# First three attentions: V as 64-column weights, the two heads of a pair on the two column halves, gates projected by channels, outputs left as operand

## The chip, the core and the metric

One core of a Trainium2 chip runs the whole program. TensorE (PE) multiplies: one operand is loaded into the array as weights, the other streams past it column by column. VectorE (DVE), ScalarE (ACT) and GpSimd (POOL) do the elementwise work, SyncE (SP) issues the loads. Each engine works through its own list in order; semaphores tie the lists together. The metric is the device time of one execution in microseconds, the median of several.

## The reference

Two blocks follow each other on 512 tokens of width 1024. The first has a context of 256 more tokens. Its layers, cut to what matters here:

```
# layer 1 (ab): h = adaln(x), hc = adaln(ctx); pp = h @ w_in, split into cq, ckv, kr, gq, gk, gv, gate
# "mla": 8 heads, 96 dims for q and k, 64 for v        "gqa": 8 heads of 64, 2 kv heads
oa = joint_dense_attention(qa, ka, va, kac, vac)        # keys: 256 context + 512 tokens
ob = joint_dense_attention(qb, kb, vb, kbc, vbc)
mix = concat([oa, ob]) * silu(g)                        # 1024 channels, context rows too
x = x + gate * (mix @ w_out)
# layer 2 (cd): "win": 8 heads of 64, 2 kv heads, a window of 3 blocks of 128 beside the context, a sink
oc = joint_window_attention(q, k, v, kc, vc, sink)      # 512 channels
od = gb * short_conv(gcv * gh, conv_w)                  # 512 channels
x = x + gate * (concat([oc, od]) * silu(g) @ w_out)

def block(qi):                                          # one attention, one block of 128 queries
    p = softmax(einsum('bqkgd,bnkd->bkgqn', qi, kk) * d ** -0.5)
    return einsum('bkgqn,bnkd->bqkgd', p, vv)
```

The second block (two more layers with the attentions "diff", "fox" and "odd", and embeddings) isn't touched.

## The kernel before

Tokens stand in tiles of 128: tiles 0 to 3 are the sequence (XT), 4 and 5 the context (CT). The program is a row of stages: in1 and up (projections), the attentions gqa and mla, out1, in2, the attention win, out2, in3, and on to the end. The modulation of later layers (modb, 32 small products of 32-row results) runs between the units of gqa and mla.

A projection is a list of chunks of up to 512 columns. A chunk's weights come in units of two slabs of 128 rows; ACT rounds a unit to a high part (L1341), POOL makes the low part (L2197), and `tile_product` (L966 to 985) does three matmuls for each slab and tile: high by high, high by low, low by high (L982 to L984). In the row form tokens are weights and the columns of w stream; in the col form columns of w are weights and 512 tokens stream, so that the result has channels on its partitions. Before, only col_b, col_c, col_h and col_z of in2 are in the col form. `turn_group` (L942) turns rows into operand columns by transposes (L949), ACT writes their high part (L1406), DVE the low one (L1813).

An attention (`attention` on each engine: L1149, L1466, L1948) is a loop over units, one head and one tile of queries. gqa and mla have 48: in each head the tiles 0, 4, 1, 5, 2, 3. A unit of tiles 0 to 3 has 768 keys (six blocks, here a large unit), one of tiles 4 and 5 has 256 (two blocks, a small unit). win has 32 units of 512 or 640 keys. Step j of the loop:

- PE: scores of unit j (L1190 and L1191, in mla L1193 to L1195) into banks 0 and 1 or 2 and 3; transposes for the operands of the next heads (L1145); transposes of the probabilities of unit j-1 (L1218), the first half of the blocks to bank 4, the rest to bank 5; the product with V of unit j-2 (L1230); then a step of modb if one is due (L1080, L1089). The weights of L1230 are the turned probabilities, 128 columns; what streams is a block of V, 64 columns, in fp32.
- DVE: the minimum of the scores (L1966, in win L1969), the low parts of operands (L1888), the copy of bank 4 (L1980), 1/sum (L1986), and result times 1/sum times gate into rows of rz (L1992).
- ACT: the exponential with its sum (L1491), and the copy of bank 5 (L1502).

Banks 4 and 5 have one buffer each: the transposes of a unit wait for the copies of the unit before it. After mla the rows in rz are turned by 48 transposes of 128 by 128 for out1 (m1), after win by 16 for out2 (m2). Two tiles of the next stage (`lead_tile`) stand among the last units to fill the array's time.

The order is written out by hand in the loops and in tables by step number.

## Time and profile before

| what | us |
| --- | --- |
| median of 3 runs | 1586.86 (1584.73 to 1588.18) |
| the profiled execution, its own time | 1588.51 |
| its span, first to last instruction | 1586.6 |
| TensorE busy in it | 1522.5 (96%) |

The profile lists each engine's busy time, the chain of work that ended last, and the instructions in order of time with what they waited for. A matmul's row runs from its start to the modelled end of its result; the next one on the array starts sooner, so what a group of matmuls occupies is read from its start to the start of the next row. An fp32 matmul stands as two records; a transpose and an fp32r matmul as one.

### The profile page before, as it was taken

Reading aid. Unit: us, or ns where it says so; the run is one execution under the profiler, and the core shown is the slowest. Engines: PE = TensorE matmul, PEld = TensorE weight load, DVE = VectorE, ACT = ScalarE, POOL = GpSimd, SP = SyncE. Lnnn points to the kernel's source line nnn. Section 1 sums busy time; section 2 is a strip of 40 time slices with the busy share of each in tenths; the row PEclk is TensorE's granted clock in tenths of the full one; section 3 lists DMA queues with packets and bytes.
Section 4 is the critical chain, followed back from the end, with each engine's and each line's share of the span. In section 5 each row is a group of like instructions: output and inputs, shape, how many; then the busy total and the mean of one; then the engine's idle time right before and its main releaser. Section 6 shows DMA issues by size and latency. Waiting matters only on the chain.

```text
span 1586.6 us, 24812 instructions
## 1 busy us (share of the span) xinstructions
PE 1522.5 (96%) x9192; PEld 1299.9 (82%) x9192; DVE 895.5 (56%) x2041; ACT 663.4 (42%) x1351; POOL 571.8 (36%) x333
## 2 busy tenths in 40 slices
PE   5999999999999999999999999987999999999998
PEld 3788978998998878888888889965788788877887
DVE  4575787666665265943752798046321599717312
ACT  3322354445554353335643424457423433336332
POOL 1232235900001553446705444421344444430244
PEclk9999999999999999999999999999999999999999
DMA  9421213331013242331003323300123233310322
GB/s 327 118 66 55 74 55 94 95 94 41 28 41 120 90 123 80 93 97 49 28 15 95 87 90 91 94 27 28 50 84 103 80 97 102 93 54 1 98 89 93
DMA packets 102630, 128.60 MB, mean 81 GB/s; under 512 B 10544, under 2 KB 60656, under 8 KB 102512
## 3 DMA queue, kind: packets, MB, share of 16 engines
q1 hardware_dynamic: 102512, 127.01, 26.4%
q8 instruction: 76, 1.25, 0.3%
q14 instruction: 42, 0.34, 0.1%
HBM read 124.90 MB, written 2.10 MB: 80 GB/s over the span
## 4 chain that ended last, share of the span: by engine, by line
PE 87%; DVE 6%; issue 3%; ACT 2%; DMA 1%; POOL 1%; SPq 1%; DVEq 0%; ACTq 0%; POOLq 0%
PE psum L982 20%; PE psum L984 20%; PE psum L983 20%; PE psum L1230 8%; PE psum L1218 4%; PE psum L949 3%; PE psum L1145 2%; PE psum L1190 1%; PE psum L1080 1%; PE psum L1197 1%; PE psum L1193 1%; PE psum L1191 1%; PE psum L1195 1%; PE psum L1194 1%; DVE psum L1910 1%
## 5 line engine op out<-in xcount | busy, mean ns | idle before, releaser
L2197 POOL TENSOR_TENSOR wlo<-wraw,whi 128x1024 fp32r<-128x1024 f32 (+4 forms) x177 | 411.6, 2326 | 906.2 <-ACT whi L1341 906.2
L1341 ACT ACTIVATE whi<-wraw 128x1024 fp32r<-128x1024 f32 (+4 forms) x177 | 180.5, 1020 | 459.3 <-PE psum L984 453.1
L982 PE MATMUL psum<-whi,h2h 128*128 128x512 f32 (+2 forms) x800 | 309.5, 387 | 2.5 <-DVE h2l L1813 1.5
L984 PE MATMUL psum<-whi,h2l 128*128 128x512 f32 (+2 forms) x800 | 305.2, 381 | 0.0
L983 PE MATMUL psum<-wlo,h2h 128*128 128x512 f32 (+2 forms) x800 | 304.6, 381 | 0.0
L982 PE MATMUL psum<-whi,hTh 128*128 128x512 f32 (+2 forms) x500 | 192.2, 384 | 3.5 <-DVE hTl L1813 2.4
L984 PE MATMUL psum<-whi,hTl 128*128 128x512 f32 (+2 forms) x500 | 186.9, 374 | 0.0
L983 PE MATMUL psum<-wlo,hTh 128*128 128x512 f32 (+2 forms) x500 | 186.6, 373 | 0.0
L982 PEld LDWEIGHTS psum<-whi,h2h 128*128 128x128 f32 x800 | 150.3, 188 | 28.4 <-issue 2.7
L984 PEld LDWEIGHTS psum<-whi,h2l 128*128 128x128 f32 x800 | 150.2, 188 | 27.1
L983 PEld LDWEIGHTS psum<-wlo,h2h 128*128 128x128 f32 x800 | 150.4, 188 | 24.7
L1491 ACT ACTIVATE pr<-psum,nmax 128x256 f32<-128x256 f32 (+6 forms) x160 | 113.3, 708 | 92.2 <-DVE nmax L1966 76.4
L982 PEld LDWEIGHTS psum<-whi,hTh 128*128 128x128 f32 x500 | 95.1, 190 | 19.7 <-issue 3.3
L984 PEld LDWEIGHTS psum<-whi,hTl 128*128 128x128 f32 x500 | 94.9, 190 | 16.6
L1966 DVE TENSOR_REDUCE nmax<-psum 128x1 f32<-128x768 f32 x96 | 74.9, 780 | 57.7 <-PE psum L1195 31.3
L983 PEld LDWEIGHTS psum<-wlo,hTh 128*128 128x128 f32 x500 | 95.3, 191 | 14.5
L1218 PE MATMUL psum<-ident,pr 128*128 128x128 f32 x672 | 102.6, 276 | 3.5 <-ACT pr L1491 3.2
L1230 PE MATMUL psum<-gq,prT 128*128 128x64 f32 x736 | 91.1, 269 | 0.0
L1230 PEld LDWEIGHTS psum<-gq,prT 128*128 128x128 f32 x736 | 88.5, 192 | 0.3 <-issue 0.2
L1218 PEld LDWEIGHTS psum<-ident,pr 128*128 128x128 f32 x672 | 76.0, 141 | 13.6 <-ACT pr L1491 10.1
L1980 DVE COPY prT<-psum 128x256 f32<-128x256 f32 (+2 forms) x160 | 73.1, 457 | 5.3 <-PE psum L1218 4.7
L1992 DVE SCALAR_TENSOR_TENSOR rz<-psum,rinv,rz 128x64 f32<-128x64 f32 (+1 forms) x160 | 47.5, 297 | 40.9 <-PE psum L1230 38.1
(321 smaller groups left out, 2609.9 us busy)
## 6 DMA issues: line engine op xcount, KB each, us to landing
wraw<-mod_w_in SPq DMA_DIRECT2D x32, 512.0 KB, 3.8
wraw<-w_in_odd_in SPq DMA_DIRECT2D x32, 512.0 KB, 3.7
wraw<-cd_w_in_in SPq DMA_DIRECT2D x24, 512.0 KB, 3.7
wraw<-w_in_even_in SPq DMA_DIRECT2D x20, 512.0 KB, 3.8
wraw<-ab_w_in_in SPq DMA_DIRECT2D x16, 512.0 KB, 4.0
wraw<-ab_w_out_in SPq DMA_DIRECT2D x16, 512.0 KB, 3.7
wraw<-w_ple_gate_in SPq DMA_DIRECT2D x16, 512.0 KB, 3.8
mod_w_even<-mod_w_in SPq DMA_DIRECT2D x8, 512.0 KB, 10.4
```

The source lines that it names most:

```text
L949: mm = eng.transpose(psum[:, b, n_ * P:(n_ + 1) * P], turn[name]["rows"](t, k), ident[:, :])
L982: eng.matmul(dst, a[0], ww[0], start=first, stop=False)
L983: eng.matmul(dst, a[0], ww[1], start=False, stop=False)
L984: mm = eng.matmul(dst, a[1], ww[0], start=False, stop=last_)
L1218: mm = eng.transpose(psum[:, bk, (b - b0) * P:(b - b0 + 1) * P], pr[:, i % 2, b * P:(b + 1) * P], ident[:, :])
L1230: mm = eng.matmul(psum[:, 6, 0:dv], prT[:, i % 2, n_ * P:(n_ + 1) * P], v_rows(name, h, b), start=n_ == 0, stop=n_ == len(bl) - 1)
L1341: eng.activation(hi_of(u)[:, :, 0:w], wraw[:, u["id"] % RAW, :, 0:w], ACT.Copy).then_inc(*to("split_hi", u["id"]))
L1491: eng.activation(pr[:, j % 2, 0:w], psum_flat[:, s0 * 512:s0 * 512 + w], ACT.Exp, bias=nmax[:, j % 4:j % 4 + 1], scale=-1.0, accum_out=rsu ...
L1966: eng.tensor_reduce(m, sc, AX.X, ALU.min).then_inc(*note("nmax", (name, j)))
L1980: eng.tensor_copy(prT[:, i % 2, 0:nb * P], psum[:, 4, 0:nb * P]).then_inc(*note("probs_a", (name, i)))
L1992: eng.scalar_tensor_tensor(out=dst, in0=o, scalar=ri, in1=dst, op0=ALU.mult, op1=ALU.mult)\
L2197: eng.tensor_tensor(lo_of(u)[:, :, 0:w], wraw[:, u["id"] % RAW, :, 0:w], f32(hi_of(u)[:, :, 0:w]), ALU.subtract)\
```

## The change

In gqa, mla and win the units are now taken by pairs of heads: head h and head h+1 of the same tile stand side by side in the list. `column_attention` takes the place of `attention` for these three:

- In the product with V, the weights are a block of V (64 columns), and the turned probabilities stream (128 columns). Head h writes partitions 0 to 63 of bank 6, head h+1 partitions 64 to 127, block by block in turn. The result has channels on its partitions. So 1/sum must lie along the columns: two more fp32 matmuls for each pair (L1300, 1/sum repeated over 64 weight columns, the identity streams) write it beside the result.
- DVE then does two multiplications of 128 by 128 per pair (gate times 1/sum, times result) in place of two of 128 by 64, and one reciprocal of two columns.
- PE turns the probabilities two steps after their scores (one before) and does the product with V of a pair at every second step, four steps after the pair's first scores. There are three buffers for probabilities and for turned ones. Bank 4 takes two blocks (three before), bank 5 up to four.
- The queries of two heads are turned by one transpose of 128 columns (two of 64 before), in gqa and win.
- The gates of layer 1 are projected by channels (form "both": 512 sequence tokens, then 256 context tokens stream past weight columns), as three chunks of 384, 384 and 256 columns, and those of win by the col form. The result of the attention is multiplied in place, and is the operand: the transposes of m1 and m2 are gone. ACT copies the high part of a pair's 128 channels (`mix_hi`, 8 of 128 by 768 and 4 of 128 by 512), POOL subtracts for the low part (`mix_lo`).
- out1 and out2 take their slabs in the order 0, 4, 6, 2 in the first chunk. After the last unit of mla nothing is turned.
- Where mla starts, eight operands are prepared ahead (four before).

```diff
         def units_of(name):
-            if name in ("gqa", "mla"):
-                return [(h, t) for h in range(8) for t in (0, 4, 1, 5, 2, 3)]
+            if name in COLUMNS:
+                return [(h, t) for h0 in range(0, 8, 2) for t in ((0, 4, 1, 5, 2, 3) if name != "win" else XT) for h in (h0, h0 + 1)]
...
# TensorE
+            def column_attention(name):
...
+                for j in range(n_units + 3):
...
+                    if (name, j) in LEAD_COLUMNS:
+                        lead_tile(*LEAD_COLUMNS[name, j])
+                    if 2 <= j < n_units + 2:
+                        turn_probs(name, j - 2, probs(name, j - 2))
+                    m, r = divmod(j - 4, 2)
+                    if m >= 0 and r == 0:
+                        h, t = units[2 * m]
+                        for e in range(2):
+                            copies_ready(name, 2 * m + e)
                         bank_free(6)
-                        for n_, b in enumerate(bl):
-                            mm = eng.matmul(psum[:, 6, 0:dv], prT[:, i % 2, n_ * P:(n_ + 1) * P], v_rows(name, h, b),
-                                            start=n_ == 0, stop=n_ == len(bl) - 1)
+                        for n_, b in enumerate(bl):
+                            for e in range(2):
+                                eng.matmul(psum[64 * e:64 * e + 64, 6, 0:P], v_rows(name, h + e, b),
+                                           turned_probs(name, 2 * m + e)[:, n_ * P:(n_ + 1) * P], start=n_ == 0, stop=n_ == len(bl) - 1)
+                        eng.wait_ge(*at("vector", ("inverse", name, m)))
+                        for e in range(2):
+                            col = rinv[:, 2 * (m % 4) + e:2 * (m % 4) + e + 1].broadcast_to([P, 64])
+                            mm = eng.matmul(psum[64 * e:64 * e + 64, 6, P:2 * P], col, ident[:, :], start=True, stop=True)
...
# VectorE
+            def column_attention(name, beside=lambda j: None):
...
+                for j in range(len(units) + 4):
+                    if j < len(units):
+                        maximum(name, j)
+                    m, r = divmod(j - 5, 2)
+                    if m >= 0 and r == 0:
+                        z = gate_columns(name, m)
+                        eng.wait_ge(*at("product_v", (name, m)))
+                        eng.tensor_tensor(z, psum[:, 6, P:2 * P], z, ALU.mult).then_inc(*small())
+                        after_last()
+                        eng.tensor_tensor(z, psum[:, 6, 0:P], z, ALU.mult).then_inc(*note("mixed", (name, m)))
+                    m, r = divmod(j - 3, 2)
+                    if m >= 0 and r == 0 and m < len(units) // 2:
...
+                        eng.reciprocal(rinv[:, r_:r_ + 2], rsum[:, c_:c_ + 2]).then_inc(*note("vector", ("inverse", name, m)))
+                    if 2 <= j < len(units) + 2:
+                        copy_probs(name, j - 2, turned_probs(name, j - 2), (name, (j - 5) // 2) if j >= 5 else None)
...
# ScalarE
+            def column_attention(name):
...
+                        exponentials(name, j, probs(name, j))
+                    if 2 <= j < len(units) + 2:
+                        copy_probs(name, j - 2, turned_probs(name, j - 2), (name, (j - 5) // 2) if j >= 5 else None)
...
+                    if (name, j) in MIX_HI:
+                        mix_hi(*MIX_HI[name, j])
```

On TensorE, in gqa, a small unit's step before: scores of unit j, transposes of the large unit j-1, the product with V of the small unit j-2 (L1230), modulation (L1089). kTs and qTs are the keys and queries of gqa, pr and prT the probabilities and the turned ones:

```order
L1190 MATMUL psum<-kTs,qTs 128x256 [waits exps]
L1191 MATMUL psum<-kTs,qTs 128x256
L1218 MATMUL psum<-ident,pr 128x128 [waits probs_a,exps]
L1218 MATMUL psum<-ident,pr 128x128 x2
L1218 MATMUL psum<-ident,pr 128x128 [waits probs_b]
L1218 MATMUL psum<-ident,pr 128x128 x2
L1230 MATMUL psum<-gq,prT 128x64 [waits mixed,probs_a]
L1230 MATMUL psum<-gq,prT 128x64
L1089 MATMUL psum<-sel,mod_row 128x2 [waits mod_rows]
```

And an even step of the changed kernel: scores of a small unit j, transposes of the large unit j-2 (L1238), the product with V of the small pair j-4, j-3 (L1295), its 1/sum (L1300), modulation (L1152); rx is a third buffer of turned probabilities:

```order
L1271 MATMUL psum<-kTs,qTs 128x256 [waits exps]
L1272 MATMUL psum<-kTs,qTs 128x256
L1238 MATMUL psum<-ident,pr 128x128 [waits probs_a,exps]
L1238 MATMUL psum<-ident,pr 128x128
L1238 MATMUL psum<-ident,pr 128x128 [waits probs_b]
L1238 MATMUL psum<-ident,pr 128x128 x3
L1295 MATMUL psum<-rx,gq 64x128 [waits mixed,probs_a]
L1295 MATMUL psum<-prT,gq 64x128
L1295 MATMUL psum<-rx,gq 64x128
L1295 MATMUL psum<-prT,gq 64x128
L1300 MATMUL psum<-ident,rinv 64x128 [waits vector]
L1152 MATMUL psum<-wraw,silu_pad 32x128 [waits evac_dve,load_w1]
```

The product with V is now in every second step only, and the transposes of unit j-2 still wait (probs_a) for DVE's copy of unit j-3.

On VectorE, in gqa, two steps before:

```order
L1966 TENSOR_REDUCE nmax<-psum 128x1 [waits evac_dve,scores]
L1980 COPY prT<-psum 128x256 [waits product_v,probs_turned]
L1986 RECIPROCAL rinv<-rsum 128x1 [waits exps]
L1992 SCALAR_TENSOR_TENSOR rz<-psum,rinv,rz 128x64 [waits product_v,vector]
L1966 TENSOR_REDUCE nmax<-psum 128x1 [waits mixed,scores]
L1980 COPY prT<-psum 128x384 [waits product_v,probs_turned]
```

and two steps of the changed kernel, even and odd:

```order
L2104 TENSOR_REDUCE nmax<-psum 128x1 [waits evac_dve,scores]
L2115 COPY rx<-psum 128x256 [waits product_v,probs_turned]
L2104 TENSOR_REDUCE nmax<-psum 128x1 [waits probs_a,scores]
L2128 TENSOR_TENSOR rz<-psum,rz 128x128 [waits product_v]
L2130 TENSOR_TENSOR rz<-psum,rz 128x128 [waits vector]
L2135 RECIPROCAL rinv<-rsum 128x2 [waits exps]
L2115 COPY prT<-psum 128x256 [waits product_v,probs_turned]
```

In an odd step two multiplications and the reciprocal now stand between the minimum and the copy; before, the copy came right behind the minimum.

## Rows read from the trace of the kernel before

**Rows 1.** Stretches: us, busy (instructions) of PE, PEld, DVE, ACT, POOL, clock, DMA, GB/s.

```profile
225.40:363.40 138.00, 134.41 (x1325) 120.55 (x1323) 96.56 (x253) 67.80 (x174) 67.67 (x77) 1.00 0.32 93
363.40:505.90 142.50, 140.45 (x1196) 131.76 (x1196) 92.73 (x232) 73.62 (x174) 4.76 (x2) 1.00 0.19 60
736.00:821.50 85.50, 80.75 (x676) 76.49 (x674) 60.89 (x174) 54.10 (x148) 45.57 (x32) 1.00 0.04 14
509.40:514.70 5.30, 5.30 (x15) 4.17 (x14) 0.69 (x1) 0.60 (x1) 0.00 (x0) 0.51 0.00 0
1040.00:1072.00 32.00, 25.44 (x146) 17.40 (x144) 19.92 (x70) 19.59 (x58) 5.59 (x5) 1.00 0.00 1
```

**Rows 2.** In order of time, TensorE in gqa: start, us, what, xrecords.

```profile
300.50 0.38 PE L1218 MATMUL psum<-ident,pr 128*128 128x128 f32 x2
300.72 1.45 PE L1230 MATMUL psum<-gq,prT 128*128 128x64 f32 x12
302.10 0.65 PE L1080 MATMUL psum<-wraw,silu_pad 128*32 128x128 f32 x16
302.68 0.38 PE L1190 MATMUL psum<-kTg,qTs 128*128 128x256 f32 x1
...
303.01 0.81 PE L1218 MATMUL psum<-ident,pr 128*128 128x128 f32 x6
303.67 0.56 PE L1230 MATMUL psum<-gq,prT 128*128 128x64 f32 x4
304.06 0.34 PE L1089 MATMUL psum<-sel,mod_row 128*128 128x2 f32 x2
304.26 0.48 PE L1190 MATMUL psum<-kTg,qTs 128*128 128x512 f32 x1
...
305.04 0.38 PE L1218 MATMUL psum<-ident,pr 128*128 128x128 f32 x2
```

**Rows 3.** The same, in mla.

```profile
412.01 1.45 PE L1230 MATMUL psum<-cq,prT 128*128 128x64 f32 x12
413.26 0.48 PE L1193 MATMUL psum<-kTh,qTh 96*128 96x512 f32 x1
...
414.41 0.82 PE L1218 MATMUL psum<-ident,pr 128*128 128x128 f32 x6
```

**Rows 4.** The same, VectorE in gqa, beside Rows 2.

```profile
300.70 0.96 DVE L1966 TENSOR_REDUCE nmax<-psum 128x1 f32<-128x768 f32 x1 [0.56 <-PE psum L1191]
301.58 0.41 DVE L1980 COPY prT<-psum 128x256 f32<-128x256 f32 x1
301.91 0.15 DVE L1986 RECIPROCAL rinv<-rsum 128x1 f32<-128x1 f32 x1
...
303.21 0.42 DVE L1966 TENSOR_REDUCE nmax<-psum 128x1 f32<-128x256 f32 x1 [0.65 <-PE psum L1191]
```

**Rows 5.** Two lines of code on VectorE: ns min/median/max, first and last start, forms.

```profile
L1992 DVE SCALAR_TENSOR_TENSOR rz<-psum,rinv,rz x160: 282/284/352, 233.8 to 1478.0; 128x64 f32<-128x64 f32 x128, 128x128 f32<-128x128 f32 x32
L1888 DVE TENSOR_TENSOR kTl<-psum,kTh x16: 411/554/689, 359.6 to 471.8; 96x512 fp32r<-96x512 f32 x8, 96x256 fp32r<-96x256 f32 x8
```

**Rows 6.** In order of time: TensorE waits for VectorE, start of gqa.

```profile
227.37 0.68 DVE L1888 TENSOR_TENSOR qTs<-psum,qTs 64x512 fp32r<-64x512 f32 x1
...
228.20 0.65 PE L1080 MATMUL psum<-wraw,silu_pad 128*32 128x128 f32 x16 [1.49 <-DVE qTs L1888]
```

**Rows 7.** In order of time, TensorE in win, a unit of five blocks.

```profile
748.36 0.36 PE L1190 MATMUL psum<-kTs,qTs 128*128 128x256 f32 x1
...
749.09 0.62 PE L1218 MATMUL psum<-ident,pr 128*128 128x128 f32 x4
```

**Rows 8.** The same, from mla's last unit to out1.

```profile
504.56 1.45 PE L1230 MATMUL psum<-cq,prT 128*128 128x64 f32 x12
...
509.41 0.78 PE L982 MATMUL psum<-whi,hTh 128*128 128x512 f32 x1
```

**Rows 9.** The same, where win ends and out2 goes on.

```profile
822.18 1.06 PE L949 MATMUL psum<-ident,rz 128*128 128x128 f32 x8 [0.54 <-DVE rz L1992]
```

More of the change, by code:

```diff
@@ L280, in proj @@
             return (w, tiles, lhs, evac), k
-        stage("in1", [proj(win1[:, a:b], ALL, "hT", ("act", (a, b))) for a, b in ((0, 512), (512, 1024), (1024, 1536), (1536, 2048), (2048, 2336))])
+        stage("in1", [proj(win1[:, a:b], ALL, "hT", ("act", (a, b))) for a, b in ((0, 512), (512, 1024), (1024, 1312))]
+              + [proj(win1[:, 1312 + k * P:1312 + (k + n) * P], list(range(2 * n)), "hT", ("act", ("z", k)), form="both")
+                 for k, n in ((0, 3), (3, 3), (6, 2))])
         wuq, wukv = io["mla_w_uq"][0], io["mla_w_ukv"][0]
@@ L594, in keys_of @@
             if name in STACKED and g == 0:
-                return kTs[:, part, a:b]
+                return (kTs if name == "gqa" else win_kT)[:, part, a:b]
             if name == "gqa":
@@ L640, in prep_times @@
                 first = next(j for j, a in enumerate(heads) if a // g == h // g - 1)
+                if name in COLUMNS:
+                    first = next(j for j, a in enumerate(heads) if a // 2 == h // 2 - 1)
                 when = max(nxt, first)
@@ L895, in _ @@
             load(rx[:, 0:NX, :], x_, "load_x", 3)
+            rest = [u for c in ST["out1"] for u in c["units"]][SPL:]
+            for u in rest[:2]:
+                weights(u)
+            eng.wait_ge(*at("product_v", ("mla", len(units_of("mla")) // 2 - 1)))
             load(rx[:, NX:NT, :], ctx_, "load_x", 4)
-            for u in [u for c in ST["out1"] for u in c["units"]][SPL:]:
+            for u in rest[2:]:
                 weights(u)
@@ L953, in _, with mixed_slab @@
             started = set()
+            def mixed_slab(name, k):
+                return next(key for key, k_ in MIXED.items() if k_ == k and (key[0] == "win") == (name == "out2"))
             def lead_tile(name, n_):
@@ L1312, in _ @@
             products("up")
-            attention("gqa")
-            attention("mla")
+            column_attention("gqa")
+            column_attention("mla")
             products("out1")
@@ L1317, in _ @@
             products("in2")
-            attention("win")
+            column_attention("win")
             products("out2")
@@ L1611, in _ @@
             products("in1", "up", beside=tables)
-            attention("gqa")
-            attention("mla")
+            column_attention("gqa")
+            column_attention("mla")
             def first_squares(where):
@@ L1949, in attention @@
+            def attention(name):
                 _, _, _, prT = temps(name)
-                units = units_of(name)
-                lag = LAG
-                preps = prep_times(name)
-                for p_ in preps[-1] if name in BEFORE and name != "gqa" else ():
+                units, preps = units_of(name), prep_times(name)
+                for p_ in preps[-1]:
                     first_head(name, p_)
-                for j in range(len(units) + lag + 1):
+                for j in range(len(units) + LAG + 1):
@@ L2129, in _ @@
                     first_head("gqa", p_)
-            attention("gqa", mla_norms)
-            attention("mla")
+            column_attention("gqa", mla_norms)
+            column_attention("mla")
             products("out1", 0)
@@ L2359, in _ @@
             mla_norms()
-            ahead("out1")
+            for pair in (("gqa", 0), ("gqa", 1), ("mla", 0), ("mla", 1)):
+                mix_lo(*pair)
+            split_lo(ahead_of("out1")[0])
+            mix_lo("mla", 2)
+            split_lo(ahead_of("out1")[1])
+            for pair in (("gqa", 2), ("gqa", 3), ("mla", 3)):
+                mix_lo(*pair)
             products("out1", then=ahead_of("in2"))
@@ L2363, in _ @@
             conv()
+            for p_ in range(3):
+                mix_lo("win", p_)
             ahead("out2")
+            mix_lo("win", 3)
             products("out2", "in3")
```

470 lines of the change are left out of this document (278 added, 192 removed), and 3 rows, old and new, of the table turns_at.

## Prediction

> **What bounds the kernel now.** I read the windows by stage first, then the rows in order of time on TensorE and VectorE, then the groups by line. [rows 1]: in gqa TensorE is busy for 134.41 of 138.00 us, in mla for 140.45 of 142.50, in win for 80.75 of 85.50. So TensorE's own list sets the time, and 3.6 + 2.1 + 4.8 = 10.4 us are its waits. VectorE is at 65 to 71 percent there, ACT at 49 to 63, POOL has 4.76 us of work in mla. Work taken from TensorE is time won as long as it then waits for nobody. That is the question of this case, since the change also alters who stands behind whom.
>
> **Product with V: off the path of TensorE.** Before, a large unit's twelve records take 302.10 − 300.72 = 1.38 us in gqa [rows 2] and 413.26 − 412.01 = 1.25 in mla [rows 3]; a small unit's four take 0.39 [rows 2]. I take 1.30 and 1.25: gqa 32 × 1.30 + 16 × 0.39 = 47.8, mla 46.2. Win has 144 blocks of 1.25 / 6 = 0.21: 30. Together 124.
>
> After, a record streams 128 columns. A record of that width takes 0.11 us as a transpose, six in 303.67 − 303.01 = 0.66 [rows 2]. Whether two column halves run side by side no row of an attention shows; the nearest is L1080, where four groups of 32 columns with all 128 rows as weights take 302.68 − 302.10 = 0.58 us for 16 records [rows 2], that is 0.145 for a round of four. One after the other they would take 16 × 0.11 = 1.8. So a round of two halves costs between 0.11 and 0.145. I take 0.11, and the rest of that row, 0.58 − 4 × 0.11 = 0.14, once for going to groups and back. The 1/sum matmuls are two rounds, 0.22. A large pair: 12 × 0.11 + 0.36 = 1.68; a small one 4 × 0.11 + 0.36 = 0.80. Two stages of 16 × 1.68 + 8 × 0.80 = 33.3, win 15.8 + 16 × 0.36 = 21.6: 88. **Saved 36** (with 0.145 for a round 13 less).
>
> The rows of L1080 show four column groups over the same 128 rows side by side. The Trainium skill ("TensorE: Matmul & The Clock Gate", Part 3: Packing small matmuls, "What overlaps and what doesn't") says that weights load beside running matmuls only when their row group differs, and both heads use all rows; by that rule the product would run one half after the other, which is rival C.
>
> **Transposes of queries.** 24 fewer in gqa, 16 fewer in win, 0.11 each: **saved 4.4**.
>
> **The new wait.** This is the term that decides. In every even step TensorE's transposes of unit j−2 go to bank 4, and wait for VectorE's copy of unit j−3. In the order of the changed kernel, VectorE makes it at the end of the odd step j−1, behind the minimum of unit j−1, two multiplications and the reciprocal. Before, it stood behind the minimum alone. The chain from the last score of unit j−1:
>
> - to the start of the minimum 300.70 − 300.50 = 0.20 (start of the next TensorE row to the start on VectorE) [rows 2, 4];
> - the large minimum 301.58 − 300.70 = 0.88; a small one 0.42 [rows 4];
> - two multiplications of 128 by 128. No row has this form. L1992 with 128 by 128 is at most 352 ns; L1888 takes 411 ns for 256 columns and 689 for 512, so 0.14 per 128 columns and 0.27 for 128 [rows 5]. Bounds 0.27 and 0.35; I take 0.30, since both operands come as in L1888: 0.60;
> - reciprocal, occupying about 0.10 beside its 0.15, and copy 0.41 [rows 4];
> - VectorE's end to TensorE's start 228.20 − 228.05 = 0.15 at most [rows 6]; 0.12 taken.
>
> Sum 2.3 us behind a large unit, 1.8 behind a small one. In that time TensorE has the transposes of unit j−3 (0.66 or 0.22), in gqa modulation (305.04 − 304.26 = 0.78 are scores, 304.26 − 304.06 = 0.20 modulation), and the scores of unit j: 0.78 large and 0.33 small in gqa [rows 2], 1.15 [rows 3] and about 0.46 in mla (0.33 × 1.15 / 0.78 gives 0.49). What is missing is the wait. The six even steps of a pair of heads in gqa, by the tiles 0, 4, 1, 5, 2, 3 of unit j: 0.67, 1.14, 0.17, 1.58, 0.17, 1.14, together 4.9. Mla: 0.53, 1.21, 0, 1.65, 0, 0.96, together 4.4. In win a chain of 2.2 meets 0.44 + 0.73 [rows 7]: 1.05 in each of four steps, 4.2. Four pairs of heads each: 19.6 + 17.4 + 16.8 = 53.8, and 1.0 for ACT's copy of bank 5, now four blocks. TensorE's preparations of operands fall into some of these waits: 32 or so transposes, 3.6 us, that cost nothing there. And with a lag of two steps the transposes no longer wait for the exponential, which I put at 3 of the 10.4 us of waits that are there. **New waits 54.8 − 3.6 − 3.0 = 48.2.**
>
> Within the three attentions then: +48.2 − 36 − 4.4 = **+7.8 us**. The work saved comes back as waiting.
>
> **Ends of mla and win.** Between mla's last product, 504.56 and 1.29 long, and the first full product of out1 at 509.41 lie 3.56 us of waits and turns [rows 8]. And the stretch behind it, twelve matmuls in 509.40 to 514.70, has a granted clock of 0.51 [rows 1], the lower level (1.2 GHz), at 0.43 each where they take 0.23 otherwise: 2.4 lost. The engine had waited for 2 us before the clock fell. Of the 48 transposes of m1, 40 lie outside that stretch: 40 × 0.11 = 4.4. Now the two tiles of out1 stand around the last pair, and nothing is turned: **−10.4**. What comes late next is the last pair of mla: product, two multiplications 0.9, ACT's high part of 768 columns about 0.9 (the exponential over 768 is near), POOL's subtraction and the low part of the weights, some 5 to 6 us, against the slabs 0, 4 and 6 of out1 ahead of slab 2: 3 × 3 × 4 matmuls of 0.23 = 8.3. Hidden, by 2 us; without that cover those 5 us return. Win: 0.54 of waiting before its eight transposes [rows 9], and 16 × 0.11 = 1.8: **−2.3**.
>
> **Added elsewhere.** The gates of in1 by channels stream 512 and then 256 columns: 192 matmuls of 256 columns in place of 96 of 512. At equal columns no more work, but for some 0.4 of starts. Four more operands ahead of mla, and the fill of a pipeline two steps longer, about 1: **+1.4**. ACT's `mix_hi` (12 pieces of at most 0.9) and POOL's `mix_lo` lie beside TensorE's work in the second half of mla and in win; ACT is at 73.62 of 142.5 there and POOL nearly idle [rows 1]. SP now holds the context load and later weights of out1 until mla's last product; two units are loaded ahead, and the rest has the 8.3 us of above.
>
> **Sum.** 7.8 − 10.4 − 2.3 + 1.4 = −3.5 us. Against the profiled execution's own 1588.51 that is 1585.0; the median lies 1.65 lower: **1583.4**.
>
> **Rivals.**
>
> A, *the waits are smaller* (faster). If the two multiplications overlap like the copy behind the minimum (0.41 long, 0.33 occupied [rows 4]) and a finished instruction is seen sooner, a chain is 0.3 us shorter. There are 24 + 24 + 16 = 64 even steps: −19 us, 1564. For it speaks that all spans of VectorE in my sum are whole durations; against it that gaps of 0.20 stand in the rows as they are, and that the chain starts anew each second step.
>
> B, *the waits are longer* (slower than before). Place: the odd step on VectorE, where the low parts of operands (0.41 to 0.69 each [rows 5], now two behind each transposed query pair) push the minimum, and the multiplications cost 0.35. Price 0.3 us in each of 64 steps: +19, 1602. It decides early: from 0.055 us per even step more than my sum the gain is gone, from 0.11 on the kernel is measurably slower. The clock could add to it: [rows 8] show waits of 2 us ahead of the fall in [rows 1]. Against the clock speaks 1040 to 1072, where TensorE is busy for only 25.44 of 32 us at clock 1.00 [rows 1], a share like the one that I expect in gqa.
>
> C, *the halves don't run side by side* (slower). Each round takes 0.22: the pairs cost (16 × 12 + 8 × 4) × 0.11 = 24.6 more in gqa and in mla, 15.8 in win, less what the waits absorb (products stand in the steps with the wait, but behind it: little). +60, 1643. L1080 speaks against it.
>
> D, *the change doesn't remove the end of mla*: POOL's or SP's chain is late and TensorE waits 5 us there again: 1588, no change.
>
> **How the numbers follow.** What this kernel's runs can tell from no change is about 0.2%, 3.2 us. The sum as it stands has 0.43 (between 1576 and 1592: 0.22 of it faster, 0.15 within, 0.06 slower), A 0.24, B 0.22, C 0.05, D 0.06. Faster 0.46, same 0.21, slower 0.33. The range from A to B with a little for the open price of a round: 1560 to 1604; C and the tails are left out.
>
> **What would show it.** In the trace after: (1) on TensorE 24 records of L1295 in about 1.3 us, or in 2.6 (C); (2) in even steps an idle of 0.2 to 1.6 us before the transposes, ended by VectorE's copy, none in odd ones; large minimum, multiplications and copy in a row behind one another on VectorE; (3) the length of a multiplication: 0.27 or 0.35; (4) TensorE busy about 40 us less in the three stages at a length within 3 percent of before; (5) out1 starting at clock 1.00 without a gap. The forecast is wrong if the transposes don't wait in even steps, if the waits stand elsewhere (ACT's copy of bank 5, the operands), or if the clock is below 1.00 in an attention.

## The result: slower by 0.65 percent

| | before | changed |
| --- | --- | --- |
| median, us (4 runs each) | 1585.8 | 1596.8 |
| ratio | | 1.0065 (1.0048 to 1.0083) |
| the profiled execution, its own time | 1588.51 | 1596.90 |
| its span | 1586.6 | 1595.1 |
| TensorE busy in it | 1522.5 | 1491.4 |

The forecast was 1583.4 and a little faster; the kernel is 11 us slower, inside the range but on the other side. TensorE is busy for 31 us less, though part of its work now runs at a lower clock (below), and the program is longer all the same. The page of the changed kernel, its line of busy times:

```profile
PE 1491.4 (93%) x9440; PEld 1244.1 (78%) x9440; DVE 860.5 (54%) x1957; ACT 670.8 (42%) x1345; POOL 592.7 (37%) x349
```

The windows of the changed kernel, to hold against [rows 1]: gqa, mla with the start of out1, win, and below them three short stretches (columns as in [rows 1]: length, busy time of PE, PEld, DVE, ACT, POOL, granted clock):

```profile
228.34:371.22 142.88, 123.10 (x1409) 100.85 (x1409) 87.73 (x227) 72.25 (x174) 67.78 (x77) 0.96 0.31 90
371.22:525.00 153.78, 133.83 (x1269) 112.94 (x1268) 81.00 (x202) 79.44 (x175) 16.85 (x9) 0.96 0.15 46
...
745.10:831.00 85.90, 73.61 (x718) 60.93 (x717) 53.58 (x155) 53.62 (x148) 49.55 (x35) 1.00 0.05 14
232.00:240.00 8.00, 6.79 (x50) 5.17 (x50) 5.36 (x9) 3.16 (x9) 3.16 (x3) 0.50 0.23 68
376.00:384.00 8.00, 6.96 (x35) 5.98 (x28) 2.88 (x6) 3.10 (x8) 0.00 (x0) 0.50 0.23 66
457.00:460.00 3.00, 3.00 (x22) 2.66 (x21) 1.37 (x3) 1.64 (x4) 0.00 (x0) 0.50 0.00 0
```

Two things stand in these rows. TensorE waits for 19.8 us in gqa (142.88 − 123.10), where it waited for 3.6 before. And the granted clock, 1.00 in every attention of [rows 1], is 0.96 in gqa and in mla: at the start of each, and at 457, TensorE runs at the lower of its two levels, 1.2 GHz. In windows of 2 us the low stretches come to 10.2, 10.2 and 3.4 us; TensorE is busy for 8.7, 8.9 and 3.4 of them. Half of the busy time is what the level costs: 4.4 + 4.4 + 1.7 = **10.5 us**.

Ahead of the low stretch of mla stands a wait, in order of time on TensorE:

```profile
372.36 0.60 PE L1217 MATMUL psum<-ident,rx 128*96 128x128 f32 x4
375.25 1.08 PE L1152 MATMUL psum<-wraw,silu_pad 128*32 128x128 f32 x16 [2.29 <-DVE kTl_more L2037]
376.26 0.79 PE L1274 MATMUL psum<-kTh,qTh 96*128 96x512 f32 x1
```

and on VectorE in that time:

```profile
371.91 1.02 DVE L2037 TENSOR_TENSOR qTl<-psum,qTh 96x512 fp32r<-96x512 f32 x2 [2.27 <-ACT qTh L1575]
372.85 0.28 DVE L2128 TENSOR_TENSOR rz<-psum,rz 128x128 f32<-128x128 f32 x1
373.16 0.29 DVE L2130 TENSOR_TENSOR rz<-psum,rz 128x128 f32<-128x128 f32 x1
373.55 0.96 DVE L2104 TENSOR_REDUCE nmax<-psum 128x1 f32<-128x768 f32 x1
374.43 0.68 DVE L2037 TENSOR_TENSOR kTl_more<-psum,kTh_more 96x512 fp32r<-96x512 f32 x1
```

The modulation product L1152 writes bank 7, and so do the turned operands. TensorE turned a key's operand at 372.36, and may write bank 7 again only when VectorE has made the low part, which stands behind the last pair's multiplications of gqa and the first minimum of mla: 2.29 us. Before, this wait was 1.5. The first product that follows takes 0.79 us where the same one takes 0.48 elsewhere: the clock has fallen. The start of gqa shows the same with 2.21 us.

Which waits there are (us in all, times, longest), in gqa:

```profile
PE psum L1238 <- DVE prT L2115: 8.7, 9, 1.4
PE psum L1217 <- DVE modc L1971: 4.2, 5, 1.5
PE psum L1152 <- DVE more_q L2037: 3.2, 2, 2.2
PE psum L1295 <- DVE rx L2115: 1.3, 1, 1.3
...
```

and in win:

```profile
PE psum L1238 <- DVE win_prT L2115: 3.8, 5, 1.0
PE psum L1238 <- DVE gate L2115: 3.0, 4, 0.9
PE psum L1238 <- DVE gains L2115: 2.1, 3, 0.9
...
PE psum L1238 <- ACT win_prT L1612: 0.6, 3, 0.2
```

Most are the wait that the prediction named, the transposes L1238 for VectorE's copy L2115. The last row is a small one for ACT, and turned out to be the more important.

### The profile page after: what moved, and what is told of

Read it like the earlier page. It is cut to its first block, busy times and chain, and to the rows that moved or that the text cites. A ratio compares the mean times of both kernels' runs of the same rounds, so it can differ in the third digit from the quotient of the medians.

```text
span 1595.1 us, 25028 instructions
## 1 busy us (share of the span) xinstructions
PE 1491.4 (93%) x9440; PEld 1244.1 (78%) x9440; DVE 860.5 (54%) x1957; ACT 670.8 (42%) x1345; POOL 592.7 (37%) x349
## 4 chain that ended last, share of the span: by engine, by line
PE 83%; DVE 10%; issue 3%; ACT 3%; DMA 1%; SPq 1%; POOL 0%; DVEq 0%; ACTq 0%
PE psum L1049 20%; PE psum L1051 20%; PE psum L1050 20%; PE psum L1295 5%; PE psum L1238 4%; PE psum L1005 2%; DVE nmax L2104 2%; PE psum L1217 2%; PE psum L1271 1%; PE psum L1152 1%; PE psum L1349 1%; PE psum L1331 1%; DVE psum L2058 1%; PE psum L1274 1%; PE psum L1272 1%
## 5 line engine op out<-in xcount | busy, mean ns | idle before, releaser
L1049 PE MATMUL psum<-whi,hTh 128*128 128x512 f32 (+2 forms) x372 | 140.1, 376 | 3.3 <-DVE hTl L1962 2.4
L1051 PE MATMUL psum<-whi,hTl 128*128 128x512 f32 (+2 forms) x372 | 136.0, 366 | 0.0
L1050 PE MATMUL psum<-wlo,hTh 128*128 128x512 f32 (+2 forms) x372 | 135.9, 365 | 0.0
L2104 DVE TENSOR_REDUCE nmax<-psum 128x1 f32<-128x768 f32 (+1 forms) x96 | 74.8, 780 | 106.1 <-PE psum L1276 58.0
L1049 PE MATMUL psum<-hTh,whi 128*128 128x512 f32 (+1 forms) x288 | 105.8, 367 | 0.0
L1050 PE MATMUL psum<-hTl,whi 128*128 128x512 f32 (+1 forms) x288 | 105.4, 366 | 0.0
L1051 PE MATMUL psum<-hTh,wlo 128*128 128x512 f32 (+1 forms) x288 | 105.3, 366 | 0.0
L1597 ACT ACTIVATE pr<-psum,nmax 128x768 f32<-128x768 f32 (+3 forms) x96 | 64.2, 669 | 63.9 <-DVE nmax L2104 48.9
L1049 PEld LDWEIGHTS psum<-whi,hTh 128*128 128x128 f32 x372 | 70.3, 189 | 15.1 <-issue 3.7
L1238 PE MATMUL psum<-ident,pr 128*128 128x128 f32 x368 | 62.2, 288 | 10.4 <-DVE prT L2115 6.9
## 6 DMA issues: line engine op xcount, KB each, us to landing
mod_w_even<-mod_w_in SPq DMA_DIRECT2D x8, 512.0 KB, 10.4
```

The lines of the kernel that those rows point to most:

```text
L1049: eng.matmul(dst, a[0], ww[0], start=first, stop=False)
L1050: eng.matmul(dst, a[0], ww[1], start=False, stop=False)
L1051: mm = eng.matmul(dst, a[1], ww[0], start=False, stop=last_)
L1238: mm = eng.transpose(psum[:, bk, (b - b0) * P:(b - b0 + 1) * P], place[:, b * P:(b + 1) * P], ident[:, :])
L1597: eng.activation(place[:, 0:w], psum_flat[:, s0 * 512:s0 * 512 + w], ACT.Exp, bias=nmax[:, j % 4:j % 4 + 1], scale=-1.0, accum_out=rsum[:, ...
L2104: eng.tensor_reduce(m, sc, AX.X, ALU.min).then_inc(*note("nmax", (name, j)))
```

## The experiments

Each kernel ran beside the kernel before on the same chip; times are medians, ratios are against the kernel before. The changed kernel itself ran only in the first set. A difference to it is one of medians, and since the median of the kernel before lay between 1584.7 and 1587.1 in the sets, it is good to about 2 us.

### One chain away: VectorE's copy first (e1)

```diff
 # VectorE, column_attention
                     if j < len(units):
                         maximum(name, j)
+                    if 2 <= j < len(units) + 2:
+                        copy_probs(...)
                     m, r = divmod(j - 5, 2)
                     # two multiplications, then the reciprocal
-                    if 2 <= j < len(units) + 2:
-                        copy_probs(...)
```

> The changed kernel, with one thing reordered on VectorE in gqa, mla and win: the copy of bank 4 comes right behind the minimum, and the reciprocal and the two multiplications behind the copy. If the wait of the even steps is what the prediction named (copy behind 0.28 + 0.29 + 0.07 us of other work), every such wait shrinks by 0.65 us: about 10 waits on the copy in gqa, 5 on the modulation's column behind it, 5 in mla and 12 in win, some 20 us in all, 1577. If the waits are only handed on (the multiplications come later and bank 6 or the low parts are waited for), under 8 us. Theory of the clock: the stretches at a granted clock of 0.50 at the start of gqa and of mla stay as they are, since no copy stands there.

Measured: 1591.5 (ratio 1.0039, 1.0026 to 1.0052), 5 us less than the changed kernel, not 20. The waits of win in this kernel:

```profile
PE psum L1238 <- ACT win_prT L1612: 3.8, 6, 0.8
PE psum L1238 <- ACT gate L1612: 2.9, 5, 0.8
PE psum L1238 <- ACT gains L1612: 2.1, 3, 0.8
PE psum L1238 <- DVE win_prT L2115: 1.0, 4, 0.4
...
```

VectorE's 8.9 us have become 2.4 (with rows of 0.9 and 0.5 not shown), and ACT's 1.0 has become 8.8. Win is 85.4 us from its first score to its last 1/sum, as in the changed kernel, to a tenth. There the wait changed its name and kept its length. What this execution wins lies in gqa, 3.6 us with the clock low as long as before, and in mla with out1 and in2, 4.3 us, about what the lower level costs less there (1.7 us in place of 6.2). The transposes of a unit go to two banks; the first is freed by VectorE's copy, the second by ACT's, and ACT's stands behind the exponential of the next unit. The changed kernel's own rows had it, one after the other:

```profile
819.97 0.41 PE L1238 MATMUL psum<-ident,win_pr 128*128 128x128 f32 x2 [0.95 <-DVE win_prT L2115]
820.58 0.55 PE L1238 MATMUL psum<-ident,win_pr 128*128 128x128 f32 x3 [0.20 <-ACT win_prT L1612]
```

TensorE waits 0.95 us for VectorE, transposes two blocks, and then waits 0.20 more for ACT. ACT's release comes 0.6 us after VectorE's, and only 0.20 is booked on it. Take VectorE's wait away and the rest comes to light.

### The waits at the starts filled (e2)

```diff
+        FILL = {("gqa", 0): 18, ("gqa", 1): 4, ("mla", 0): 18, ("mla", 1): 8, ("mla", 25): 10}
 # TensorE, column_attention, ahead of the modulation
+                    if (name, j) in FILL:
+                        keep_clock(FILL[name, j])      # that many transposes of the identity into bank 6
```

> The changed kernel, with TensorE given useless transposes of the identity (0.11 us each) in the stretches where it waits at the start of gqa (18 and 4), of mla (18 and 8) and in mla's step 25 (10). Nothing else moves. Theory of the clock: the three stretches at clock 0.50 (10.2, 10.2 and 3.4 us, in which TensorE was busy for 8.7, 8.9 and 3.4) come at 1.00, which gives back half of their busy time, 4.4 + 4.4 + 1.7 = 10.5 us, less 1 for transposes that outlast a wait: 1587. Rival, that the waits of the even steps alone make the kernel slower and the slow stretches were covered by waits for VectorE anyway: 1594 to 1597.

Measured: 1591.1 (1.0034, 1.0022 to 1.0046), 5.7 us less than the changed kernel although TensorE does more. Its windows:

```profile
232.00:236.00 4.00, 3.31 (x36) 2.59 (x28) 3.13 (x6) 1.90 (x5) 1.77 (x2) 1.00 0.45 132
376.00:384.00 8.00, 6.73 (x53) 5.98 (x52) 4.21 (x10) 4.81 (x12) 0.00 (x0) 1.00 0.23 66
414.00:420.00 6.00, 5.96 (x50) 5.46 (x51) 1.76 (x5) 1.87 (x5) 0.00 (x0) 0.72 0.00 0
500.00:504.00 4.00, 3.99 (x36) 3.03 (x37) 0.81 (x2) 1.89 (x6) 2.25 (x2) 0.57 0.02 6
```

The starts are at 1.00, but this execution shows the lower level at three other places instead, at 237, 415 and 500, for 3.4 us each. Low time over gqa, mla and out1's start is 10.2 us in place of 23.9, and the busy time that it costs 5.1 in place of 10.6: a difference of 5.5. That the medians differ by 5.7 doesn't confirm this size, for the profiled execution is the slowest of its seven. It took 1595.49, only 1.4 less than the changed kernel's; gqa is 1.1 us shorter, mla with out1 and in2 0.9. So some 3.5 of the 5.5 were taken back, by what isn't shown (the useless transposes themselves are a candidate). The clock's part shows between the executions: the one at 1.000 took 1589.35 us, the one at 0.994 took 1595.49. It is real, then, but the filling gives back 5.7 us by the median, and 7.5 in the one execution at 1.000, of the 10.5 that were worked out. What failed in the expectation is that filling three places would keep the clock up everywhere.

### The modulation away from the operands' bank (e3)

```diff
-            every = 2 if name == "gqa" else 6
-            n_, r = divmod(j, every)
+            n_, r = divmod(j, 2)
+            if name == "mla":
+                places = (8, 10, 20, 22, 32, 34, 36, 38)
...
```

> The changed kernel, with the eight modulation products of mla moved from steps 0, 6, 12, ... to steps 8, 10, 20, 22, 32, 34, 36, 38, where no operand is prepared in bank 7, which both use. If the waits for the low parts of operands ahead of modulation (L1152 and L1161, 2.3 + 2.6 + 1.8 + 1.5 us in mla) come from that shared bank, they go, and with them the slow clock at 457: 6 to 9 us less, 1589. If TensorE at the start of mla would have waited for the first exponential all the same, the clock falls there as before, and 2 to 4 us are won.

Measured: 1589.9 (1.0019, 1.0010 to 1.0028), 6.9 us less. The clock is at 1.00 at the start of mla, and low at 399.0 for 3.4 us instead; low time falls from 23.9 to 13.7 us, its cost from 10.6 to 6.1. That is 4.5 of the 6.9 us. The waits were moved more than removed: TensorE now waits for the same low parts ahead of the next operand's transposes (L1220, 4.9 and 2.6 us in mla; in the changed kernel the same waits were 3.0 and 1.5). Not tried: the modulation's results in the free half of bank 6, since TensorE would then write a bank that VectorE may be reading. (The Trainium skill, "PSUM — Partial Sum Buffer", section "PSUM bank collisions raise a hardware error", names two engines on the same bank and the same 32 partitions a collision; no run here shows one.)

### The three together (e4)

> The three edits together (copy first, useless transposes in steps 0 and 1 of gqa and mla, modulation of mla moved). If the even-step wait and the clock are separate causes, their gains add: about 20 + 9 + 2, 1566, below the kernel before. If they are one (fewer waits alone keep the clock up), the sum is well under that, 1575.

Of e2's fillings this kernel has those of steps 0 and 1, not the ten transposes of mla's step 25.

Measured: 1585.1 (0.9989, 0.9979 to 0.9999), 11.8 us less than the changed kernel. The single edits gave 5.3 + 5.7 + 6.9 = 17.9. They don't add, since the second and the third share the clock of mla's start, and since the first had only uncovered ACT's chain.

### Both chains away (e5)

e1, and on ACT:

```diff
 # ACT, column_attention
+                    if 2 <= j < len(units) + 2:
+                        copy_probs(...)
                     if j < len(units):
                         exponentials(name, j, probs(name, j))
-                    if 2 <= j < len(units) + 2:
-                        copy_probs(...)
```

> The edit of e1 (VectorE's copy right behind the minimum) and the same on ACT: the copy of bank 5 comes ahead of the exponential of step j. In e1 the waits for VectorE's copy of win fell from 8.9 to 2.4 us, but waits for ACT's copy rose from 1.0 to 8.8: the next chain. If that is all that was behind it, most of 8.8 in win, 2.8 in gqa and 1.6 in mla goes: e1's 1591.5 less 10 is 1581. Rival: the exponential, now behind a copy, becomes the late one, for the scores two steps on and for the transposes: 1589 to 1594.

Measured: **1572.3** (0.9907, 0.9890 to 0.9923). 24.5 us less than the changed kernel, 19 less than e1. The clock has next to no part in the 19: the medians of the granted clock are 0.9925 here and 0.992 in e1. All the waits of this kernel's win on the copies:

```profile
PE psum L1238 <- DVE win_prT L2115: 1.5, 4, 0.7
PE psum L1238 <- DVE gate L2115: 1.1, 3, 0.6
```

No wait for ACT's copy is left, and win is 75.4 us from first score to last 1/sum, 10 less than in e1.

### ACT's copy alone (e9)

> The changed kernel with ACT's copy of bank 5 ahead of the exponential, and VectorE's order as it is. Theory of two chains side by side: in the changed kernel's even steps VectorE's copy comes first as the cause of a wait, ACT's 0.15 to 0.2 us after it; taking away ACT's alone brings only that remainder, 1 to 4 us, 1593 to 1596, while both together brought 24 (e5). If ACT's order was the whole cause (the exponentials come too late for something else), it brings most of the 19 us between e1 and e5: 1578.

Measured: 1586.4 (1.0004, 0.9995 to 1.0014), 10.4 us less than the changed kernel, more than the 1 to 4 of the expectation. Win is 80.8 us, 4.6 less; low clock is down to 13.6 us, its cost to 6.2 (4.4 less). The profiled execution has 0.995, as high a clock as any of its ten; their median is 0.993, so the clock's part in the 10.4 is rather less than 4.4. I had priced the edit by the 0.15 to 0.2 us that the profile books on ACT in a step, and the steps gave 0.3. The four kernels make a square:

| | VectorE as changed | VectorE's copy first |
| --- | --- | --- |
| ACT as changed | 1596.8 | 1591.5 |
| ACT's copy first | 1586.4 | 1572.3 |

Alone the edits bring 5.3 and 10.4, together 24.5.

### All edits (e6 and e10)

e5 with e4's edits, 14 more transposes of the identity in step 2 of gqa, and 20 in place of 18 in its step 0.

> e4 with ACT's copy ahead of the exponential too, and fourteen more useless transposes in gqa's step 2, where e4 still had 3.4 us of slow clock behind a wait of 1.8. If gains add: e4's 1585.0 less 10 (ACT's chain) less 1.7 (clock) is 1573, below the kernel before by 14. If ACT's order brings nothing, 1583.

Measured: **1565.5** (0.9867, 0.9850 to 0.9883), 20.6 us below the kernel before. The windows of gqa and of win:

```profile
229.00:361.00 132.00, 121.09 (x1440) 101.33 (x1440) 87.48 (x228) 72.71 (x174) 67.63 (x77) 1.00 0.33 97
...
726.00:802.00 76.00, 71.05 (x719) 61.53 (x717) 54.96 (x154) 55.09 (x148) 50.07 (x36) 1.00 0.06 15
```

Gqa is 132.5 us to mla's first score (361.92 − 229.43) at clock 1.00, where the changed kernel takes 142.9 and the one before 138.

e10 is e6 with VectorE's low parts ahead of its multiplications:

> e6 with VectorE's low parts of prepared operands right behind the copy, ahead of the reciprocal and the two multiplications. In e6 TensorE waits in mla for bank 7 until these low parts are made, 4.1 + 2.6 + 1.1 + 0.6 + 0.4 us, and 3.6 for the modulation's column behind them. In odd steps they stand behind 0.65 us of other work; that half of the waits shrinks: 2 to 5 us less, 1562. Rival: the multiplications are then late for bank 6, and nothing is won, 1565.

```diff
 # VectorE, column_attention, behind the copy and ahead of the multiplications
+                    for p_ in preps.get(j, []):
+                        low(name, p_)
```

Measured: 1563.7 (0.9862, 0.9845 to 0.9878). Against e6's 0.9867 that is no difference that can be told: the intervals cover each other. It is the fastest kernel of the study by its median, 1.4 percent below the kernel before.

### Is it the clock? The kernel before, made to wait (e7, and e8 with the wait filled)

```diff
 # the kernel before, VectorE, low parts of operands, in step 0 of gqa and mla only
+                if twice:
+                    eng.tensor_tensor(lows[0], shaped(turned, lows[0]), f32(highs[0]), ALU.subtract).then_inc(*small())
+                    after_last()
                 eng.tensor_tensor(lows[0], shaped(turned, lows[0]), f32(highs[0]),
                                   ALU.subtract).then_inc(*note("heads_lo", (name, p_[0])))
```

> The kernel before, in which VectorE makes the low part of the operands of step 0 of gqa and of mla twice, so that TensorE waits about 2.15 us at the start of the two attentions in place of 1.5, as it does in the changed kernel. Theory of the clock: the longer wait lets the clock fall to 0.50 for about 10 us in each, and the kernel loses 2 x (0.7 + 4.4) = 10 us: 1597. Rival: the length of this wait isn't what makes the clock fall (the emptier steps behind it are): 1.4 us, 1588.

> e7 with 18 useless transposes of TensorE in each of the two waits, as in e2. Clock at 1.00 in both starts by either theory; 1588, that is the longer wait alone, 1.4 us over the kernel before.

Measured: 1591.4 for the longer wait (1.0033, 1.0023 to 1.0043), 1587.1 with the same wait filled (1.0006, 0.9996 to 1.0016). The same two windows, first without and then with the filling:

```profile
232.00:246.00 14.00, 14.00 (x84) 12.55 (x84) 8.42 (x18) 3.33 (x9) 4.40 (x3) 0.50 0.19 57
374.00:378.00 4.00, 3.66 (x29) 3.12 (x30) 1.38 (x4) 1.23 (x5) 0.00 (x0) 0.57 0.31 88
```

```profile
232.00:246.00 14.00, 13.14 (x124) 11.50 (x122) 12.68 (x25) 5.75 (x14) 5.87 (x4) 1.00 0.32 92
374.00:378.00 4.00, 4.00 (x33) 3.79 (x33) 2.50 (x9) 2.32 (x7) 0.00 (x0) 1.00 0.02 4
```

A wait of 2.21 and one of 2.22 us in place of 1.5 each: 5.3 us slower, of which the waits themselves are 1.0 (the filled kernel) and the clock 4.3. In the profiled execution, the slowest of the ten, the lower level lasted 17 us in gqa with TensorE busy nearly throughout, but only 3.4 in mla, behind the same wait. Over all ten the granted clock is 0.9945 without the filling and 0.999 with it. So the clock can fall behind a wait of 2.2 us, and does so often enough to cost 4 us in the median; how long it stays low isn't set by the wait alone. What sets it stays open. The cost of about 4 is less than the 8.8 that I expected, and the ten executions lie between 1588.7 (clock 0.997) and 1594.3 (0.991), the profiled one.

### Is the gain the order's alone? The kernel before with ACT's copy first (e12)

> A control: the kernel before, with the order on ACT of e5 (the copy of bank 5 ahead of the exponential) in gqa, mla and win. If that order is worth something by itself, the kernel before gains as well, and the 20 us of e6 aren't owed to the changed kernel. If it is worth something only where the probabilities are turned two steps after their scores, nothing is won here: with a lag of one step the transposes of unit j wait for the exponential that the copy now delays by up to 0.5 us. The step has room for some of it, so 1587 to 1600, slower rather than faster.

Measured: 1586.6 (0.9998, 0.9988 to 1.0008), no change. The kernel before, in which the transposes come one step after the scores and each unit has its own product, wins nothing by ACT's order, and VectorE's copy stands right behind the minimum there already. So the largest part of e6's 20 us is the changed kernel's saved work, which its own orders let through. Whether the fillings and the moved modulation alone would bring the kernel before something wasn't measured; with its clock at 0.999 in most executions little is left for them.

### Rival C on purpose: the heads one after the other (e11)

```diff
-                        for n_, b in enumerate(bl):
-                            for e in range(2):
+                        for e in range(2):
+                            for n_, b in enumerate(bl):
                                 eng.matmul(psum[64 * e:64 * e + 64, 6, 0:P], v_rows(name, h + e, b), ...)
```

> The changed kernel with the products of a pair in another order: all blocks of the first head, then all of the second, so that neighbours in TensorE's list share a column half. If two column halves run side by side only when neighbours differ, a large pair takes 24 x 0.11 = 2.64 us in place of 1.36, and as these products stand behind the waits of the even step, nearly all of it is felt: 24.6 + 24.6 + 15.8 = 65 us less a few, about 1655. That is the rival C of the prediction, made on purpose. If TensorE looks further ahead, 1597.

Measured: 1630.7 (1.0283, 1.0266 to 1.0301), 34 us more than the changed kernel, half of what C's price said. A large pair of this kernel:

```profile
309.85 1.20 PE L1295 MATMUL psum<-prT,gq 128*64 128x128 f32 x9
310.78 0.32 PE L1295 MATMUL psum<-rx,gq 128*64 128x128 f32 x1
310.88 0.27 PE L1295 MATMUL psum<-prT,gq 128*64 128x128 f32 x1
...
312.45 0.65 PE L1152 MATMUL psum<-wraw,silu_pad 128*32 128x128 f32 x16
```

It takes 312.45 − 309.85 = 2.60 us, and so do the others at full clock, to 0.03. The first head's last records alternate with the second head's first, so the two column halves overlap for a few records even so. In the changed kernel, where the halves alternate all the way:

```profile
498.66 1.53 PE L1295 MATMUL psum<-prT,cq 128*64 128x128 f32 x24
500.02 0.39 PE L1300 MATMUL psum<-ident,rinv 128*64 128x128 f32 x4
500.33 0.50 PE L1274 MATMUL psum<-kTh_more,qTh_more 96*128 96x512 f32 x1
```

24 records of 128 columns in 1.36 us, 0.11 a round of two, and 0.31 for 1/sum. The order thus costs 0.9 us in a large pair. On the program it costs more than the 34 us, since this kernel lost less to the clock: its four executions have 0.992 to 0.998, the changed kernel's 0.990 to 0.994, and in the profiled one the lower level costs 3.4 us in gqa and mla in place of 10.5.

That is the other thing in this trace. The start of mla has the very wait of the changed kernel, and the clock stays up behind it:

```profile
388.26 0.65 PE L1152 MATMUL psum<-wraw,silu_pad 128*32 128x128 f32 x16 [2.29 <-DVE kTl_more L2037]
```

```profile
384.00:394.00 10.00, 6.34 (x57) 5.22 (x54) 5.80 (x12) 5.19 (x13) 0.00 (x0) 1.00 0.18 53
```

So do the starts of gqa in e5, e9 and this kernel, behind 2.2 us each; in all three the clock falls only behind the wait of 1.8 that follows in step 2. And in e12, the kernel before but for ACT's order, it fell to the lower level for 3.4 us at the start of mla, behind its usual 1.50. The length of a single wait raises the risk and doesn't decide it.

## Why the prediction was wrong, by its own steps

By stages, in us of the profiled executions (the terms of the prediction for all three attentions together, −5.6, are split evenly here):

| stage | predicted | measured | difference |
| --- | --- | --- | --- |
| in1 and up | +1.4 | +2.9 | +1.5 |
| gqa | +0.6 | +4.9 | +4.3 |
| mla, out1, in2 | −7.8 | +1.5 | +9.3 |
| win and on | +2.4 | −0.9 | −3.3 |
| sum | −3.4 | +8.4 | +11.8 |

**Product with V: right.** A large pair was to take 1.68 us and takes 1.67 (500.33 − 498.66), a small one 0.80 and takes 0.81. L1080 was the right row for two column halves. By the rule of the Trainium skill ("TensorE: Matmul & The Clock Gate", Part 3: Packing small matmuls, "What overlaps and what doesn't") weights of the same rows would not load beside running matmuls. Both heads use all 128 rows, and the trace shows rounds of two in 0.11, so the measurement decides against that rule here.

**The new wait: right in total, wrong in its parts.** Waits rose by 16.2 us in gqa (17.7 predicted) and by 17.9 in mla (15.5). The chain on VectorE was well sized: in the changed kernel's gqa, in order of time,

```profile
290.30 0.96 DVE L2104 TENSOR_REDUCE nmax<-psum 128x1 f32<-128x768 f32 x1 [2.29 <-PE psum L1272]
291.17 0.28 DVE L2128 TENSOR_TENSOR rz<-psum,rz 128x128 f32<-128x128 f32 x1
291.49 0.29 DVE L2130 TENSOR_TENSOR rz<-psum,rz 128x128 f32<-128x128 f32 x1
291.70 0.15 DVE L2135 RECIPROCAL rinv<-rsum 128x2 f32<-128x2 f32 x1
291.77 0.40 DVE L2115 COPY prT<-psum 128x256 f32<-128x256 f32 x1
```

```profile
292.32 0.85 PE L1238 MATMUL psum<-ident,rx 128*128 128x128 f32 x6 [0.90 <-DVE prT L2115]
```

0.20 + 0.87 + 0.53 + 0.07 + 0.40 + 0.15 = 2.22 us, against 2.3. Three parts of the step were wrong. First, I let the preparations of operands "cost nothing" inside those waits. They have a chain of their own, bank 7: the low parts, which before stood right behind the minimum and now stand behind the multiplications and the copy. In mla TensorE waits about 15 us for bank 7 and 5 for the copies, where I had 17.4 for the copies. Second, I gave ACT's chain 1.0 us in all, as an addition to VectorE's, when it is a chain beside it and the longer one: e1 shows it. Third, in win the waits are 7.5 us more than before, not 15: in the twelve steps that have one it is 0.7 us on average by the copy (8.9 / 12), and four of the sixteen even steps have none. That is where the forecast was too high, by the −3.3 of the last row.

**The clock: the step that failed.** In "Ends of mla and win" I took a gain of 2.4 from the clock, and under rival B I wrote that it "could add to it", and argued it away with the stretch of [rows 1] that is busy for 25.44 of 32 us at 1.00. A mean share over 32 us says nothing of a single wait. The row that mattered was beside it in [rows 6]: TensorE waits 1.49 us at the start of gqa, for a low part, ahead of modulation. The change lengthens just this wait, by twice as many low parts in one step and by a step without a product to cover it. I had even counted the four more operands (in the 1 us of fill), but as work and not as a wait. And the row that I took for a wait of 2 us ahead of the fall is two: TensorE waited 0.54 us, did four transposes at 506.54, and waited 1.50; the clock fell at 507.8, inside the second, of which 0.6 us had passed. In the profiled execution of the changed kernel the lower level then cost 10.5 us, against 11.8 by which the sum missed. e7 against e8 shows that such waits alone make the clock fall, at a price of 4.3 us for two of them; e2 shows that with them filled the loss at those places is gone. What the experiments give back is less than the 10.5, 5.7 by e2's median, and even its execution at clock 1.000 is 6 us over the forecast. So the cause is shown, and its full size is worked out from the rows of one execution, which has the median's time and clock.

**The 2.4 us of the end: a term of one execution.** The low stretch behind mla in [rows 1] was there in the profiled execution, whose mean granted clock was 0.996. Of the 70 executions of the kernel before that ran beside these kernels, 48 had 0.999, and the start of the program accounts for that missing thousandth:

```profile
0.00:50.00 50.00, 30.03 (x291) 23.59 (x292) 21.51 (x60) 16.57 (x36) 7.60 (x8) 0.97 0.88 293
```

50 × 0.03 / 1587 is 0.001. So most executions can't have had the stretch of 6.8 us behind mla that the profiled one had (this is from their mean clock alone). One of half the length isn't excluded, since the start isn't low in every execution: e12's profile has none there and one of 3.4 us at 510. The profiled execution was 1.65 us over its median, and the change couldn't win against the median what the median didn't lose. The rest of the term was real: out1 starts without a gap and at 1.00.

**In1: under-sized.** A matmul of 256 columns takes 0.12 us and one of 512 takes 0.23, so that two halves cost 0.01 more than one whole: 96 of them 1.0, not 0.4. Of the 2.9 measured 1.9 remain, where the sum had 1.0 for operands and fill. A wait of 0.69 for the first operand of up is part of it; the rest stays open.

**Rival B** came true in its sign and nearly in its size (1602 against 1596.8), by a mechanism that it only mentioned. The even step was not longer than the sum had it. What the rival had right is its decision point: 0.055 us per even step were enough to turn the sign, and a sum of −3.5 us from terms of 48, 36, 12 and 4 had no sign to speak of.

## What to carry to other kernels

Where two engines each free a bank for the same consumer, the profile names the one that ends the first wait, and what it books on the other is only the remainder: price both chains from their start, and move both (5 and 10 us alone, 24 together here). Put an engine's copy that frees a buffer ahead of its work for the next step as soon as the transposes it reads come a step earlier. A wait of about 2 us on TensorE costs more than itself, since the clock may fall behind it; look for the longest single wait that a change makes, at starts of stages first, and fill it. Then look again, for the clock may fall behind a later one (e2). And hold a profiled execution's granted clock against that of the other runs before a stretch at a low clock is entered in a sum.

## What the runs showed of the hardware

- Two column halves with all 128 rows each run side by side when neighbours in TensorE's list alternate between them: 24 fp32 records of 128 columns in 1.36 us. With one half's twelve records ahead of the other's, the pair with its 1/sum takes 2.60 us in place of 1.67.
- The clock fell behind waits of 2.2 to 2.3 us at the start of a stage (the changed kernel, e7), behind one of 1.8 in step 2 of gqa (e4) and behind ones of 1.5 at 456 (the changed kernel) and at the start of mla (e12). It did not behind others of 1.4 to 1.5, nor behind 2.22 and 2.29 at the starts of gqa and mla in e11. No length of a wait decides it in these runs. Low stretches in these attentions lasted from 3.4 to 17 us, the longest with TensorE busy nearly throughout (e7).
- Over the 70 executions of the kernel before, a mean granted clock lower by a thousandth goes with 1.0 us more, in a wide scatter: the 48 at 0.999 lie between 1584.4 and 1587.5. The changed kernel's four executions had 0.990 to 0.994 (median 0.9905). An estimate by that slope, carried beyond the range of 0.995 to 1.000 that it comes from, makes the 0.0085 to 0.999 worth 8 us, most of the 11 between the medians.
- Matmuls of 256 columns 0.12 us, of 512 columns 0.23.
